# An expert's rows gathered to 96 of 128 partitions, three of every four, and put in order by the row transposes

## The reference

```python
logits = jnp.dot(x2, w_router) + b_router
top_val, top_idx = lax.top_k(logits, TOP_K)          # 4 of 32
gates = jax.nn.softmax(top_val, axis=-1)
...
def block_fn(args):                                  # the rows of one expert
    e, rows = args
    xb = x2[rows]
    gu = jnp.dot(xb, w_gu[e]) + b_gu[e]
    gate, up = gu[:, :EXPERT_FF], gu[:, EXPERT_FF:]
    gate = jnp.minimum(gate, SWIGLU_LIMIT)
    up = jnp.clip(up, -SWIGLU_LIMIT, SWIGLU_LIMIT)
    hmid = gate * jax.nn.sigmoid(SWIGLU_ALPHA * gate) * (up + 1.0)
    return jnp.dot(hmid, w_down[e]) + b_down[e]
...
y = jax.ops.segment_sum(y_rows * sorted_gate[:, None], sorted_tok, num_segments=N)
```

## Time and profile before

| what | value |
|---|---|
| median of three runs | 1379.21 us (1378.73 to 1381.3) |
| the profiled execution's own time | 1379.13 us |
| its span in the profile | 1377.4 us |
| TensorE busy, weight load busy | 1284.2 us (93%), 881.0 us (64%) |
| VectorE, ScalarE, GpSimd busy | 1008.3 us (73%), 680.5 us (49%), 121.9 us (9%) |
| DMA, mean over the span | 343 GB/s; in the slices of the experts' loop 398 to 416 |
| mean granted TensorE clock | 0.973 of full |
| gather: issue to landing, median | 10.7 us, 32 of them |

### The profile page before, as it was taken

One profiled execution on the slowest core, in us unless ns is written; L12 is line 12 of the kernel. 1 busy time (PEld: TensorE's weight loads), 2 busy tenths in 40 slices (PEclk: granted clock), 3 DMA queues, 4 the chain that ended last, 5 costly groups with the idle time before them and its releaser, 6 DMA issues.

```text
span 1377.4 us, 34698 instructions
## 1 busy us (share of the span) xinstructions
PE 1284.2 (93%) x15188; PEld 881.0 (64%) x15188; DVE 1008.3 (73%) x1575; ACT 680.5 (49%) x814; POOL 121.9 (9%) x139
## 2 busy tenths in 40 slices
PE   6999999858999999999999999999999999999955
PEld 3446645446777776666677777776666676776722
DVE  4542436558888888888778888878887887888866
ACT  4431221145556556565556656556555665655511
POOL 1000811010000000000000000000000000000002
PEclk9999999959999999999999999999999999999987
DMA  9640154088999999999999999999999999999982
GB/s 319 225 170 1 64 190 207 23 314 315 403 410 414 409 412 411 412 403 406 411 408 410 406 412 413 408 415 414 414 398 410 408 411 411 414 413 412 406 350 71
DMA packets 50005, 472.60 MB, mean 343 GB/s; under 512 B 8541, under 2 KB 9332, under 8 KB 24636
## 3 DMA queue, kind: packets, MB, share of 16 engines
q1 hardware_dynamic: 38860, 436.22, 78.0%
q0 software_dynamic: 10336, 31.77, 6.5%
q10 hardware_dynamic: 656, 2.36, 0.5%
HBM read 446.43 MB, written 29.95 MB: 346 GB/s over the span
## 4 chain that ended last, share of the span: by engine, by line
PE 59%; DMA 12%; DVE 6%; issue 2%; ACT 1%; DVEq 0%; POOLq 0%
PE wide L853 43%; PE bank L853 15%; DMA ring<-in_w_gu 9%; DVE work L1519 3%; DMA work<-part_rows 2%; PE bank L1097 1%; DMA work<-h_rows,work 1%; ACT work L781 1%; DVE ring L1627 0%; DVE ring L1625 0%; DVE ring L1614 0%; DVE work L1445 0%; DVE work L1489 0%; DVE work L1492 0%; ACT work L786 0%
## 5 line engine op out<-in xcount | busy, mean ns | idle before, releaser
L1519 DVE SCALAR_TENSOR_TENSOR work<-ring,work 128x1024 f16<-128x1024 f32 x512 | 591.1, 1219 | 127.8 <-ACT work L781 127.7
L853 PE MATMUL wide<-ring,work 128*96 128x512 f32 (+4 forms) x1400 | 564.6, 562 | 1.5 <-ACT work L718 1.0
L781 ACT ACTIVATE work<-ring 128x1024 f16<-128x1024 f32 x512 | 503.8, 1050 | 76.1 <-DMA ring<-in_w_gu 69.4
L853 PEld LDWEIGHTS wide<-ring,work 128*96 128x96 f32 (+4 forms) x1400 | 214.4, 156 | 321.1 <-issue 297.0
L853 PE MATMUL wide<-work 128*128 128x96 f16 (+1 forms) x6262 | 302.5, 210 | 36.8 <-DMA work<-part_rows 17.4
L853 PEld LDWEIGHTS bank<-work 128*128 128x128 f16 (+4 forms) x6430 | 294.4, 101 | 33.4 <-issue 23.3
L853 PEld LDWEIGHTS wide<-work 128*128 128x128 f16 (+1 forms) x6262 | 278.0, 98 | 57.3 <-issue 22.6
L853 PE MATMUL bank<-work 128*128 128x96 f16 (+4 forms) x6430 | 298.5, 209 | 9.8 <-ACT work L754 3.8
L786 ACT ACTIVATE work<-work 128x384 f32<-128x384 f32 x64 | 33.5, 524 | 199.9 <-DVE work L1492 199.9
L795 ACT ACTIVATE work<-wide,work 96x1024 f32<-96x1024 f32 x30 | 33.2, 1106 | 119.3 <-PE wide L853 119.3
L581 POOL DMA_INDIRECT work<-h_rows,work x32 | 31.8, 995 | 504.9 <-PE bank L1097 475.8
(11 more groups left out here) (190 smaller groups left out, 609.8 us busy)
## 6 DMA issues: line engine op xcount, KB each, us to landing
ring<-in_w_gu SPq DMA_DIRECT2D x128, 2048.0 KB, 23.9
ring<-in_w_down SPq DMA_DIRECT2D x64, 2048.0 KB, 28.1
part_rows<-work POOLq DMA_DIRECT2D x1, 10240.0 KB, 36.8
ring<-in_w_in SPq DMA_DIRECT2D x4, 2048.0 KB, 14.0
ring<-part_rows SPq DMA_DIRECT2D x3, 2560.0 KB, 28.5
ring<-in_w_out SPq DMA_DIRECT2D x2, 2048.0 KB, 9.5
h_rows<-work POOLq DMA_DIRECT2D x1, 2560.0 KB, 9.9
ring<-h_rows SPq DMA_DIRECT2D x1, 2560.0 KB, 22.3
```

The source lines that it names most:

```text
L781: act.activation(whi[u % BUFS], packed(s, u), ACT.Copy, scale=W_UP).then_inc(hi_done, 1)
L853: return pe.matmul(out, w, x, start=start, stop=stop, skip_group_check=True)
L1519: dve.scalar_tensor_tensor(wlo[u % BUFS], packed(s, u), W_UP, whi[u % BUFS], ALU.mult, ALU.subtract).then_inc(split_done, 1)
```

## The change

The gather takes 128 places, one for each partition, and of every four partitions the last is never used, which leaves 96. The constant `used` is a permutation: its column 3g + d picks partition 4g + d for d = 0, 1, 2, and its last 32 columns pick the unused partitions. The row transposes take it in place of the identity, so the 96 used rows come out as columns 0 to 95 as before; each writes 128 columns, and the next overwrites the last 32 of them. The ranks are dealt anew: with partition = 64a + 32b + 8c + 4e + d, rank - 1 = 32d + 16(b xor e) + 8a + 2c + e. Any sixteen successive ranks (a block with d and b xor e fixed) meet each combination of a, c, e once and each combination of a, b, c once. The table is made for 128 places and copied to `found`; `tok_i` comes from that, and a new product with `used` brings the table into the order of the 96 places, from which a new function `places_of` computes the destination. The scatter still reads 96 rows from partitions 0 to 95. `iota16` moves to a place that is free only after the router, so it and `used` are filled by eleven VectorE operations ahead of `onehot(0, 0)`. `end_hot` moves from expert 30 to behind the loop, since its tile moved too.

```diff
@@ the tiles
-        iota16 = take(BLK // 2).bitcast(F16)
...
-        hot = take(TILES * BLK // 2).bitcast(F16).rearrange("p (t s) -> p t s", t=TILES)
+        hot = take(TILES * P // 2).bitcast(F16).rearrange("p (t s) -> p t s", t=TILES)
+        found = [take(4) for _ in range(ROW_BUFS)]
         slots = [take(8)[0:BLK, :] for _ in range(ROW_BUFS)]
-        tok_i = [take(1).bitcast(I32)[0:BLK, :] for _ in range(ROW_BUFS)]
+        tok_i = [take(1).bitcast(I32) for _ in range(ROW_BUFS)]
...
-        xg = take(D)[0:BLK, :]
+        xg = take(D)
+        used = take(P)
...
+        iota16 = half_at(A + 2304 + 20 * BLK + PLACES // 2, P)
@@ TensorE, table
-                    last = mm(bank[0][0:BLK, 480:484], hot[0:n, t, :], info[0:n, t, bass.ds(e, 1), :],
+                    last = mm(bank[0][:, 480:484], hot[0:n, t, :], info[0:n, t, bass.ds(e, 1), :],
@@ TensorE, rows
             def rows(m, q, got, tables):
+                pe.wait_ge(table_copied, tables)
+                if not isinstance(m, int) or m > 0:
+                    pe.wait_ge(dst_known, m)
+                mm(bank[0][0:BLK, 484:488], used[:, 0:BLK], found[m % ROW_BUFS if isinstance(m, int) else 0], True, True)\
+                    .then_inc(sel_ready, 1)
                 pe.wait_ge(gathered[q], got)
-                pe.wait_ge(table_copied, tables)
                 for b in range(2):
                     for k in range(4):
-                        last = pe.transpose(bank[b][:, k * BLK:(k + 1) * BLK],
-                                            xg[:, (4 * b + k) * P:(4 * b + k + 1) * P],
-                                            ident[0:BLK, 0:BLK])
+                        last = pe.transpose(bank[b][:, k * BLK:k * BLK + P],
+                                            xg[:, (4 * b + k) * P:(4 * b + k + 1) * P], used)
                     last.then_inc(gT_ready, 1)
@@ VectorE, the constants: at the start before, ahead of onehot(0, 0) after
-            step(dve.tensor_copy(iota16.rearrange("p (a k) -> p a k", a=16),
-                                 iota1[:, 0:BLK].rearrange("p (k a) -> p a k", a=16)))
...
+            step(dve.memset(iota16, -1.0))
+            four = ident.rearrange("p (g d) -> p g d", d=4)
+            step(dve.tensor_copy(used[:, 0:BLK].rearrange("p (g d) -> p g d", d=3), four[:, :, 0:3]))
+            step(dve.tensor_copy(used[:, BLK:P].rearrange("p (g d) -> p g d", d=1), four[:, :, 3:4]))
+            from_rank = iota1[:, 0:BLK].rearrange("p (d x a c e) -> p d x a c e", d=3, x=2, a=2, c=4)
+            to_place = iota16.rearrange("p (a b c e d) -> p a b c e d", a=2, b=2, c=4, e=2)
+            for b in range(2):
+                for odd in range(2):
+                    for a in range(2):
+                        step(dve.tensor_copy(to_place[:, a, b, :, odd, 0:3].rearrange("p c d -> p d c"),
+                                             from_rank[:, :, b ^ odd, a, :, odd]))
@@ VectorE, rows_of
-                dve.tensor_copy(slots[q][:, 0:4], bank[0][0:BLK, 480:484]).then_inc(table_copied, 1)
+                dve.tensor_copy(found[q], bank[0][:, 480:484]).then_inc(table_copied, 1)
                 dve.wait_ge(table_copied, m + 1)
-                dve.tensor_scalar(tok_i[q], slots[q][:, 3:4], W_UP, float(PLACES), ALU.mult, ALU.add)\
+                dve.tensor_scalar(tok_i[q], found[q][:, 3:4], W_UP, float(PLACES), ALU.mult, ALU.add)\
                    .then_inc(rows_known, 1)
+            def places_of(m, q):
+                dve.wait_ge(sel_ready, m + 1)
+                dve.tensor_copy(slots[q][:, 0:4], bank[0][0:BLK, 484:488]).then_inc(slots_copied, 1)
+                dve.wait_ge(slots_copied, m + 1)
                 dve.tensor_scalar(dst_f, slots[q][:, 3:4], W_UP, float(PLACES + TOPK * SPAN), ALU.mult, ALU.add)\
...
@@ VectorE, the loop over the experts
-                if n == E - 2:
-                    dve.wait_ge(tok_known, 1)
-                    end_hot(0)
-                    end_hot(1)
...
                 if n + 1 < E:
                     rows_lo(n + 1, (n + 1) % 2)
+                    places_of(n + 1, (n + 1) % ROW_BUFS)
                     for u in range(BUFS):
                         lo(n + 1, u, piece_slot(n + 1, u // 4))
+            dve.wait_ge(tok_known, 1)
+            end_hot(0)
+            end_hot(1)
             dve.wait_ge(gates_hi, 1)
```

More of the change, by code:

```diff
@@ L79, in build @@
         ring = ctx.enter_context(nc.sbuf_tensor("ring", [P, RING * SLOT], F32))
-        work = ctx.enter_context(nc.sbuf_tensor("work", [P, 20408], F32))
+        work = ctx.enter_context(nc.sbuf_tensor("work", [P, 20440], F32))
         bank = [ctx.enter_context(nc.psum_tensor(f"bank{i}", [P, 512], F32)) for i in range(4)]
@@ L99, in take @@
                 cursor[0] += n
-                assert cursor[0] <= 20408, cursor[0]
+                assert cursor[0] <= 20440, cursor[0]
             return work[:, at:at + n]
@@ L185, in build @@
         cursor[0] = A + KT * TOK
-        hot = take(TILES * BLK // 2).bitcast(F16).rearrange("p (t s) -> p t s", t=TILES)
+        hot = take(TILES * P // 2).bitcast(F16).rearrange("p (t s) -> p t s", t=TILES)
+        found = [take(4) for _ in range(ROW_BUFS)]
         slots = [take(8)[0:BLK, :] for _ in range(ROW_BUFS)]
-        tok_i = [take(1).bitcast(I32)[0:BLK, :] for _ in range(ROW_BUFS)]
+        tok_i = [take(1).bitcast(I32) for _ in range(ROW_BUFS)]
         dst_i = [take(1).bitcast(I32)[0:BLK, :] for _ in range(ROW_BUFS)]
         dst_f = take(1)[0:BLK, :]
+        gatesT = work[BLK:P, cursor[0]:cursor[0] + PLACES]
         tok_row = take(PLACES)[0:BLK, :]
-        gatesT = work[BLK:P, cursor[0]:cursor[0] + PLACES]
-        xg = take(D)[0:BLK, :]
+        xg = take(D)
+        used = take(P)
         def half_words(n, a):
@@ L229, in build @@
         val_one = take(E * (MAXB - 1))
+        hot30 = half_at(cursor[0], PLACES)
+        take(PLACES // 2)
         g2n, b2n = ring[:, 0:D], ring[:, D:2 * D]
@@ L291, in build @@
         table_copied, dst_found, dst_known = sem("table_copied"), sem("dst_found"), sem("dst_known")
+        sel_ready, slots_copied = sem("sel_ready"), sem("slots_copied")
         gathered = [sem(f"gathered{i}") for i in range(2)]
@@ L1527, in _ @@
             rows_lo(0, 0)
+            places_of(0, 0)
             lo(0, 3, piece_slot(0, 0))
@@ L1592, in _ @@
                     rows_lo(b + E, 0)
+                    places_of(b + E, 0)
                     for u in range(16):
```

4 lines of the change are left out of this document (1 added, 3 removed).

## The result

The changed kernel takes 1385.74 us (median of 14 runs), the kernel before beside it 1380.91 us (14 runs): a ratio of 1.0029, with a 95% interval of 1.0016 to 1.0043. It is slower by 0.29%, and above the forecast range. The profiled run took 1386.42 us, its span is 1384.7 us, 7.3 us over the span of before.

The account below looks back on a forecast made before the run. TensorE was taken to bound the kernel up to expert 22, DMA the last eight experts. Loop +5.0, start +1.6 and end -14.8 gave -8.2 us, from 1379.13 to 1370.9; forecast's own range 1365 to 1378, overall 1363 to 1383.

Parts of the forecast that it names:

- The gather: Gather into 128 partitions: wins back the whole 1.0 us of DMA per expert, DMA's period falling from 32.2 to about 31.2.
- B: Rival: half of the gather's dearness goes, DMA at 31.7 us per expert, end -8 to -10, 1376.7 us; chance 0.10.
- A: Rival: the gather stays as dear as it is, only the start's cost remains, 1382.2 us (1380.5 to 1384); chance 0.24.
- TensorE per expert: Wider transposes and the added product on TensorE's list: +0.29 us per expert, bounds 0.15 to 0.45.
- D: Rival: TensorE pays more, the new product waiting each time; breaks even at x = 0.56 us per expert, 1383 at 0.7; chance 0.04.
- The start: Up to the first down: eleven small operations and slower first steps, less the gather's gain of 1.5: +1.6 us, +0.5 to +3.5.
- The loop: All 30 expert periods bound by TensorE at 32.06 us, "issue" gaps unchanged: +5.0 us, bounds +0.8 to +9.9.
- Rival C: TensorE's "issue" gaps, perhaps instructions late through full DMA engines, shrink as DMA rests: -8 more, 1363 us; chance 0.07.
- The end: After down(30): DMA has no weights left, last quarter lands at T + 35, `total` at T + 40: -14.8 us (14 to 15.3).
- The sum: Whole kernel: 5.0 + 1.6 - 14.8 = -8.2 us, giving 1370.9; with all bounds -14 to -0.6.

Follow-up runs that it names:

- old_place: The changed kernel with rows gathered to partitions 0 to 95 and ranks dealt the old way, all other operations kept: 1382.75 us, ratio 1.0028.
- before_nop128: The kernel before with 128 empty TensorE instructions, which the build dropped, so a repeat of the kernel before: ratio 0.9999.
- after_again: The changed kernel itself, unaltered, run and profiled again: ratio 1.0039 to the kernel before.
- the pads: Either kernel with 128 or 64 empty TensorE instructions with semaphore steps before the first gathered rows: before 1.0040 or 1382.98 us, changed 1.0042 or 1383.34 us.
- unit_pad: The kernel before with four empty instructions with a semaphore step behind each of 16 TensorE units of an expert: 1480.5 us, one run.
- filler_after: The changed kernel with one useless 512 KB DRAM to DRAM copy per expert, from expert 2 on: 1386.57 us, ratio 1.0038.
- light_before: The kernel before with a quarter of each piece of weights not loaded from expert 2 on: ratio 0.9939.

## Why the prediction was wrong, point by point

**The gather: right.** Dips gone (418 and 416 GB/s against 309 and 340), old_place brings them back (369 and 299). By the means over 20 experts above, the stretches from 4 to 12 us lost (26 + 115 + 92 + 21) x 2 / 427 = 1.2 us before and 0.2 us after, so the gain is the 1.0 us that was taken. The Trainium skill's "DMA: Bandwidth & Descriptors", section "The descriptor swizzle", where a transfer over 128 partitions gives each engine its own eight, agrees with this: spreading the rows over all partitions did it, with the same scattered reads. Half of the dearness (B) or all of it staying (A) are both refuted as accounts of the gather.

**TensorE per expert: right.** 0.30 us measured, 0.29 predicted; eight transposes 0.93 us, 0.88 predicted. D's reason is refuted: nothing waits for the new product. But D's x was the added time per expert, and with the gaps the loop grew as x = (14.7 + 3.7) / 30 = 0.61 has it, over D's mark of 0.56, for a reason that D did not name.

**The start: mis-sized in the one profile, about right over several.** In the profiled pair `down(0)` is 5.5 us late. The eleven operations are in the chain of the kernel after as

```profile
282.26 0.22 DVE work L1435
282.73 0.20 DVE work L1442
...
284.33 0.21 DVE work L1442
284.56 0.91 DVE work L1464 x5
```

from 282.06 to 284.56, 2.5 us against 2.3 predicted. Gather 0 took 11.04 us in place of 11.67; the step had 1.5 us for this. Then TensorE stood idle for 3.1 us behind VectorE's split (2.3 before), and the granted clock fell to half, which the earlier trace rows have as 0.5:

```profile
322.00:326.00 4.00, 1.68 (x22) 1.69 (x23) 3.90 (x8) 1.24 (x2) 0.00 (x0) 0.67 0.62 258
326.00:330.00 4.00, 4.00 (x40) 4.00 (x38) 1.77 (x5) 0.95 (x2) 0.00 (x0) 0.50 0.94 299
```

In before's profile the clock was 1.00 in both stretches; but in before_nop128 the second had 0.59, and in after_again both had 1.00. So this loss of up to 3 us is no mark of the change. Without the pads, `down(0)` starts at 324.7, 328.8, 327.8 before (mean 327.1) and 330.2, 329.2, 330.2 after (329.9): +2.8 us, against +1.6 with bounds of 0.5 to 3.5. What the term had wrong is the gather's gain, 0.6 us and not 1.5; the rest of the 5.5 is spread between executions, and the first profile of before was at its lucky end.

**The loop: the step that failed.** The step was "The 'issue' gaps stay, as nothing here touches what feeds them". The waits for weights went as predicted (4.7 us behind the split to 0.6), and 30 x 0.30 = 9.0 us came as predicted, but issue went from 10.7 + 1.0 = 11.7 to 22.0 us. Together TensorE's waits grew from 16.4 to 22.6 us, where they should have shrunk. So the loop is 14.7 us longer and not 5.0, with a mean period of 32.41 us and not 32.1. Over five executions of each kernel, pads with them, the loop means are 957.5 and 971.3 us: +13.7. Something did touch what feeds TensorE: its instructions come by DMA packets too, and DMA that is ahead of the work runs dry and starts anew in most experts, just ahead of where the units behind `down` use up instructions fastest (52 matmuls in 2 us there, 6 in `down`, by the stretches above). What is shown: the gaps go with the arrival of code packets (unit_pad, and the times of the packets), and with TensorE's list left as it is, more DMA work shortens them (filler_after, old_place) and less lengthens them (light_before). What stays open is why DMA that ran dry makes the code late. After a restart the rate is 279 to 377 GB/s in the four stretches of 1 us from 442 to 446 at a share of 0.70 to 1.13, so the loads' packets take longer. The code packets don't: in the loop they take 0.96 us in the changed kernel and 1.06 in the kernel before, and a gap ends 2.3 us after its packet's start in the one and 2.4 in the other. So it is the start of the code packet that comes late, and no view shows what holds it back.

Rival C looked at the right thing, code that comes late by DMA, and had the sign wrong: rest for DMA made the gaps grow.

**The end: right in kind, mis-sized by 2 us.** DMA has no weights left at T = 1316.38, as predicted; stretches of the kernel after:

```profile
1312.00:1316.00 4.00, 4.00 (x11) 1.50 (x10) 2.28 (x3) 0.00 (x0) 0.00 (x0) 1.00 0.02 8
1316.00:1320.00 4.00, 4.00 (x90) 3.78 (x89) 1.41 (x2) 3.58 (x4) 0.00 (x0) 1.00 0.71 230
```

The last quarter lands at 1333.87 + 20.04 = 1353.91 = T + 37.5, not T + 35, and `total` begins at 1358.7 = T + 42.3, not T + 40. The bytes at 428 GB/s take 33.1 us, so 4.4 us are lost. The first four us run at 230 GB/s, which loses (428 - 230) x 4 / 428 = 1.9 us, and for that the term had its allowance of 2 us. It had nothing for the tail, where the engines finish one after another:

```profile
1348.00:1352.00 4.00, 0.96 (x4) 0.32 (x4) 3.96 (x3) 0.77 (x1) 0.00 (x0) 0.84 0.80 339
1352.00:1356.00 4.00, 2.04 (x3) 0.97 (x4) 3.87 (x1) 0.00 (x0) 0.00 (x0) 0.50 0.06 19
```

That is (428 - 339) x 4 / 428 = 0.8 us and nearly all of the last 1.9. So the mis-sized part of this term is the tail, and it is not the gaps' cause over again. Over the five executions of each kernel the mean end is 94.8 and 82.7, -12.1 us.

**The sum.** By the means of five: 13.7 in the loop, -12.1 at the end, and 1.3 at the start (2.8 without the pads) give +2.9 to +4.4 us, where the medians have 1385.74 - 1380.91 = +4.8. In the profiled execution the forecast of 1370.9 is missed by 15.5 us: some 3.9 at the start, 9.7 in the loop and 2.0 at the end. The measured ratio on the forecast's base is 1.0029 x 1379.13 = 1383.1 us, within rival A's 1380.5 to 1384, but by luck, as A's gather that stays dear is refuted. The gain in DMA was real. It bought an end 12 us earlier, but TensorE's added work (9 us) and its late code (6 us) cost as much and more before it.

## What to carry to other kernels

Where two resources are near their limit and one is relieved, ask what that one now does in the time it wins: a DMA queue that fills a ring of slots can run dry, as here at the end of `down` in most experts. DMA time saved is only worth what the last part of the kernel can use; before that, a steady queue with a small lag was better than an early one, and holding the lead back until the last experts, with the constants made on GpSimd, came out 0.5% under the kernel before. Never write "nothing touches what feeds them" of an engine's issue gaps: its instructions are DMA traffic like any other.

## What the runs showed of the hardware

- Instructions arrive as 16 KB packets, 123 for the changed kernel, one for about 256 instructions of TensorE, and its larger issue gaps (0.5 to 1.8 us, some 20 to 30 in 960 us) end about 2.4 us after such a packet starts.
- Less traffic made the loop slower: with a quarter of the weights not loaded the loop took 966.0 us in place of 957.6.
- DMA that had run dry gave 297 to 369 GB/s in the mean of 20 experts from two to six us after `down`'s end at a busy share of 0.93 to 1.00 (changed kernel and light_before), against 422 to 429 in steady work.
- Rows of 4 KB gathered to 96 partitions took 1.0 us per expert from the other transfers that the same rows spread evenly over 128 didn't.
- Eight products of 32-bit values with 96 columns took 2.00 us with the small product for the table, eight transposes with 128 columns 0.93 us.
- 64 empty instructions with a semaphore step per expert cost 111.5 / 30 = 3.7 us each expert, four fifths of it in gaps (79 in place of 26), 70 of which end 1.5 to 3.2 us after a code packet's start.
